# Latent queries and keys of a mixer: one eviction on VectorE, latent keys and values between the latent queries, and the rotation of a head tile in the tick of its norm

## What is computed

```python
proj = h @ w_in
q_g, k_g, v_g, q_lat, kv_lat = jnp.split(proj, IN_OFFSETS, axis=-1)
q_g = apply_rope(rms_norm(q_g.reshape(B, S, 8, 64), gqa_q_norm), cos_g, sin_g)
k_g = apply_rope(rms_norm(k_g.reshape(B, S, 2, 64), gqa_k_norm), cos_g, sin_g)
o_g = blocked_attention(q_g, k_g, v_g)                  # 8 heads over 2 key heads
c_q = rms_norm(q_lat, mla_q_norm)                       # 256 latent features
q_m = (c_q @ w_q_b).reshape(B, S, 8, 96)                # 64 plain + 32 rotated
c_kv = rms_norm(kv_lat[..., :128], mla_kv_norm)
k_rope = apply_rope(kv_lat[..., 128:], cos_m, sin_m)
kv = (c_kv @ w_kv_b).reshape(B, S, 8, 128)              # 64 of key, 64 of value per head
o_m = blocked_attention(q_m, [kv keys, k_rope], kv values)
```

## Time and profile before

| | |
|---|---|
| median of 3 runs | 2328.31 us (2326.7 to 2329.49) |
| profiled execution, first to last instruction (span) | 2324.8 us |
| median of the runs less that span (start and end around it; the profile gives no further time of its execution) | 3.5 us |
| TensorE busy | 2281.0 us, 98% of the span |
| VectorE busy | 1332.0 us, 57% |
| ScalarE busy | 879.5 us, 38% |
| GpSimd busy | 230.2 us, 10% |
| mean granted TensorE clock | 0.995 |

### The profile page before, as it was taken

How to read it: one execution, slowest core, us unless ns; L and a number is a source line. 1 busy time by engine, 2 the same in 40 slices (tenths; PEclk the granted TensorE clock), 3 DMA queues, 4 the chain that set the end, 5 groups by cost and what they waited for, 6 DMA issues and landing times.

```text
span 2324.8 us, 28515 instructions
## 1 busy us (share of the span) xinstructions
PE 2281.0 (98%) x10988; PEld 1640.0 (71%) x10988; DVE 1332.0 (57%) x2055; ACT 879.5 (38%) x1518; POOL 230.2 (10%) x190
## 2 busy tenths in 40 slices
PE   8999999999999999999999999999999999999998
PEld 7755876344675587644467788888888778888886
DVE  5676654233667665432357657777335665877722
ACT  4475542121447554221142234444223234444321
POOL 2212201000221220100000010000001002000000
PEclk9999999999999999999999999999999999999999
DMA  5301439999530143999963233333334423333331
GB/s 178 97 6 39 169 142 388 410 410 410 193 102 5 35 138 145 383 410 410 410 269 109 79 93 91 100 100 92 99 100 136 114 68 91 102 97 100 103 97 46
DMA packets 112085, 381.62 MB, mean 164 GB/s; under 512 B 16464, under 2 KB 17232, under 8 KB 111696
## 3 DMA queue, kind: packets, MB, share of 16 engines
q1 hardware_dynamic: 108208, 366.80, 44.9%
q0 software_dynamic: 2304, 8.39, 0.9%
q10 hardware_dynamic: 1440, 4.62, 0.5%
HBM read 363.51 MB, written 6.29 MB: 159 GB/s over the span
## 4 chain that ended last, share of the span: by engine, by line
PE 88%; DVE 6%; ACT 3%; DMA 1%; POOL 1%; issue 1%; SPq 0%; POOLq 0%; DVEq 0%; ACTq 0%
PE ps L1361 11%; PE ps L1363 11%; PE ps L1362 11%; PE ps L1668 9%; PE ps L1385 5%; PE ps L1387 5%; PE ps L1386 5%; PE ps L1690 5%; PE ps L1549 3%; PE ps L1405 3%; PE ps L1404 3%; PE ps L1406 3%; PE ps L1499 2%; PE ps L1507 2%; PE ps L1700 1%; PE ps L1701 1%
## 5 line engine op out<-in xcount | busy, mean ns | idle before, releaser
L2480 DVE TENSOR_TENSOR wlo<-stage,whi 128x1024 fp32r<-128x1024 f32 x262 | 329.4, 1261 | 279.0 <-ACT whi L1807 278.4
L1361 PE MATMUL ps<-hTh,whi 128*128 128x512 f32 x1120 | 441.1, 394 | 0.0
L1363 PE MATMUL ps<-hTh,wlo 128*128 128x512 f32 x1120 | 436.2, 389 | 0.0
L1362 PE MATMUL ps<-hTl,whi 128*128 128x512 f32 x1120 | 436.0, 389 | 0.0
L1807 ACT ACTIVATE whi<-stage 128x1024 fp32r<-128x1024 f32 x262 | 276.0, 1057 | 328.3 <-PE ps L1387 120.6
L1361 PEld LDWEIGHTS ps<-hTh,whi 128*128 128x128 f32 x1120 | 210.3, 188 | 48.1 <-issue 4.7
L1363 PEld LDWEIGHTS ps<-hTh,wlo 128*128 128x128 f32 x1120 | 210.2, 188 | 43.9
L1362 PEld LDWEIGHTS ps<-hTl,whi 128*128 128x128 f32 x1120 | 210.4, 188 | 42.5
L2395 DVE TENSOR_TENSOR ps<-ps,Rs 128x512 f32<-128x512 f32 x124 | 86.1, 699 | 139.2 <-PE ps L1363 125.2
L2398 DVE SCALAR_TENSOR_TENSOR t<-ps,vecs,t 128x511 f32<-128x511 f32 (+1 forms) x176 | 131.1, 745 | 3.8 <-ACT t L1770 0.7
L2395 DVE TENSOR_TENSOR x<-x,ps 128x512 f32<-128x512 f32 x184 | 116.5, 681 | 28.4 <-PE ps L1387 18.0
(11 more groups left out here) (382 smaller groups left out, 4281.5 us busy)
## 6 DMA issues: line engine op xcount, KB each, us to landing
stage<-in_wpk SPq DMA_DIRECT2D x268, 512.0 KB, 3.6
wa<-in_wd SPq DMA_DIRECT2D x56, 512.0 KB, 15.5
wa<-in_wu SPq DMA_DIRECT2D x54, 512.0 KB, 13.0
wa<-in_wg SPq DMA_DIRECT2D x46, 512.0 KB, 13.9
ws<-in_wg SPq DMA_DIRECT2D x26, 512.0 KB, 10.7
ws<-in_wu SPq DMA_DIRECT2D x24, 512.0 KB, 10.8
wr<-in_wg SPq DMA_DIRECT2D x24, 512.0 KB, 15.2
stage<-in_wd SPq DMA_DIRECT2D x22, 512.0 KB, 16.1
```

The source lines that it names most:

```text
L1361: pe.matmul(o, h, ah, start=k == 0, stop=False)
L1362: pe.matmul(o, h, al, start=False, stop=False)
L1363: t = pe.matmul(o, lo, ah, start=False, stop=k == 7)
L2480: ve.tensor_tensor(M.wlo[i % NW][:, :], M.stage[i % NSTAGE][:, :], f(M.whi[i % NW][:, :]), ALU.subtract).then_inc(*S.wlo.mark(("w", i)))
```

## The change

Chunk 12 is split, and its load issued, before the tick that norms q1 instead of after it. The order of the latent part becomes: two latent queries, a tick, the four key pairs, two value tiles, a tick, two value tiles, two latent queries, a tick, two latent queries, a tick, one latent query, high part of key head 0, the last latent query, low part and copy of key head 0. A latent query is evicted by one VectorE instruction over all 128 partitions; the table `mcs` gets ones in its upper half once. The rotation of k, q0, q1 and q2 goes into `last` instead of `later`. The cosine product on GpSimd is a step of its own right behind the swap, with two buffers in turn. Key head 0 is no longer split behind the first two score tiles.

```diff
-EARLY = {0: ("k", 0), 1: ("k", 0), 2: ("q0", 0), 3: ("q0", 0), 4: ("q0", 1), 5: ("q0", 1), 6: ("k", 1), 7: ("k", 1)}
+EARLY = {2: ("q0", 0), 3: ("q0", 0), 4: ("q0", 1), 5: ("q0", 1), 6: ("k", 1), 7: ("k", 1)}
...
                     self.do("head_swap", l, tile)
+                    self.do("head_cos", l, tile)
...
                     if tile == "q3":
                         self.last.append(lambda: self.last.append(lambda: self.last.append(st3)))
                     else:
-                        self.later.append(st3)
+                        self.last.append(st3)
...
         self.do("point", "hdone", l)
+        i0, i1 = self.chunk(1), self.chunk(1)
         self.do("mk_rope", l, 0)
         self.tick()
...
-        i0, i1 = self.chunk(1), self.chunk(1)
-        for h in range(8):
+
+        def latent_q(h):
             u = self.take()
             self.do("mq", l, h, u, i0, i1)
             self.drop(u)
-            if h in (1, 4, 7):
-                self.tick()
-        self.rel |= {i0, i1}
+        latent_q(0)
+        latent_q(1)
+        self.tick()
         i = self.chunk(0)
         for p in range(4):
             u = self.take()
             self.do("mk", l, p, u, i)
             self.drop(u)
-        self.tick()
         for p in range(1, 4):
             self.do("mk_rope", l, p)
         for m in range(NT):
             u = self.take()
             self.do("vm", l, m, u, i)
             self.drop(u)
+            if m == 1:
+                self.tick()
         self.rel.add(i)
+        for h in range(2, 8):
+            latent_q(h)
+            if h in (3, 5):
+                self.tick()
+            if h == 6:
+                self.do("head_hi", l, "k", 0)
+        self.do("head_lo", l, "k", 0)
+        self.do("key_dup", l, 0)
+        self.rel |= {i0, i1}
...
-        elif name == "mq":
-            l, h, u, i0, i1 = a
-            q.wait_ge(*S.pe.at("mq", l, h))
-            copy(M.mq[0:64, h, :], M.ps[u[0]][0:64, :], ("mq", l, h), ("free",) + u, scale=96 ** -0.5)
...
-            if i:
-                q.wait_ge(*S.dve.at("head_rot", l, HEADS[i - 1]))
-            gp.tensor_tensor(M.tmp[3][:, :], M.raw[SLOT[tile]][:, :], M.cosg[:, :], ALU.mult).then_inc(
+            if i > 1:
+                q.wait_ge(*S.dve.at("head_rot", l, HEADS[i - 2]))
+            else:
+                q.wait_ge(*S.dve.at("krope", l))
+            gp.tensor_tensor(M.tmp[2 + i % 2][:, :], M.raw[SLOT[tile]][:, :], M.cosg[:, :], ALU.mult).then_inc(
...
+            if l == 0:
+                ve.memset(M.mcs[0:64, :], 1.0).then_inc(*S.dve.mark(("mcs",)))
...
-            stt(M.mq[64:128, h, :], M.ps[u[0]][64:128, :], 96 ** -0.5, M.mcs[64:128, :], ALU.mult, ALU.mult, ("mq", l, h),
-                ("free",) + u)
+            q.wait_ge(*S.dve.at("mcs"))
+            stt(M.mq[:, h, :], M.ps[u[0]][:, :], 96 ** -0.5, M.mcs[:, :], ALU.mult, ALU.mult, ("mq", l, h), ("free",) + u)
```

More of the change, by code:

```diff
@@ L1492, in pe_program @@
                 g = 2 * (p - 4) + h
-                q.wait_ge(*S.act.at("mq", l, g))
                 q.wait_ge(*S.dve.at("mq", l, g))
@@ L2208, in pool_program @@
             power(M.st[:, 16 + 4 * g:20 + 4 * g], 4, ("pow", l, "o%d" % g))
-        elif name == "head_rot":
+        elif name == "head_cos":
             l, tile = a
@@ L2592, in dve_program @@
             after_own()
-            tt(M.raw[s][:, :], M.tmp[3][:, :], M.sq[s][:, :], ALU.add, ("head_rot", l, tile))
+            tt(M.raw[s][:, :], M.tmp[2 + HEADS.index(tile) % 2][:, :], M.sq[s][:, :], ALU.add, ("head_rot", l, tile))
         elif name == "head_lo":
```

## The result

The changed kernel takes 2351.3 us (median; 2348.3 to 2355.8) where the kernel before takes 2327.5 us beside it: a ratio of 1.0101, interval 1.0089 to 1.0113. The forecast was 2348.3 us and slower. The profiled execution took 2348.34 us with a span of 2346.3 us, 21.5 us more than before; the other runs have spans of 2348.7 to 2353.8.

A forecast was written before the change was run, and what follows sets the result against it. TensorE, busy 98% of the span, was taken as the bound. Span 2324.8 plus 3.5 around it plus (9.5 - 1.2) x 2 = 16.6 gave 2344.9; a clock fall of 3.4 made 2348.3 us, range 2338 to 2356.

The forecast's parts named there:

- The sum: Whole kernel: scores 9.5 us later, less 1.2 us from the key head, in 2 layers, plus 3.4 us of clock.
- Steps 1 and 2: Layer 0, swaps of k and q0: VectorE waits 3.9 us each; TensorE loses nothing, then 0.6 us in latent query 0.
- Step 3: Layer 0, chunk 12's split ahead of norm q1: norm starts at 89.85, TensorE idles 2.7 us before the transposes.
- Step 4: Layer 0, swap of q1 behind a load and key copy: starts at 91.0, landed at 94.9; norm q2 at 97.6.
- Steps 5 and 6: Layer 0, value tiles wait for banks; tile 3 idles TensorE 4.5 us behind q2's swap; scores begin at 113.45, 9.5 us later.
- The clock: Latent part: idle TensorE brings one fall to 0.50 in each layer, costing 1.7 us a layer, 3.4 us in all.
- The key head: Start of the scores: splitting key head 0 ahead of them gains 1.2 us a layer, bounds 0.5 and 2.0.
- The evictions: Latent queries: dropping ScalarE's 16 halves and widening VectorE's instruction to 128 partitions is worth nothing.
- The clock holds: Rival for the latent part: no fall of the clock, all else as forecast, 2344.9 us; chance 0.31.
- Only q1 and q2 show: Rival: the early two swap waits are absorbed, norm q1 comes at 87.4, stall 2.45 us smaller, 2340.0 us; chance 0.10.
- The banks hide it: Rival: TensorE's eight banks hide the swap waits, 4.4 us faster, 2323.9 us; chance 0.05.
- no difference: Rival: a swap near 2 us in the new place, 3.2 us slower in all, 2331.5 us; chance 0.06.

The follow-up runs named there:

- The late split: Changed kernel with chunk 12 split after the tick that norms q1, as before the change; rotations stay in the tick of their norm: 2342.4 us, ratio 1.0064.

## Why the prediction was right, by its steps

**The sum.** Forecast: (9.5 - 1.2) x 2 + 3.4 = 20.0 us on the span. Measured: 10.6 + 11.6 later scores, less 1.07 + 1.09, is 20.1. The span is 1.5 us above the 2344.8 that this makes of it; the median lies 3.0 us above the forecast, as the profiled execution was the quickest of the four. Two of the other three executions show a mean granted clock of 0.990 and 0.991, this one 0.994, so more time at the low clock may be part of that; they have no trace, and it stays open. The total is closer than its terms, which err in both directions; that they cancel is luck.

**Steps 1 and 2** hold. Norm k ends at 72.47 and its swap has landed at 76.48, 4.0 us; q0's took from 80.36 to 84.33, the same 4.0, against the 3.9 assumed. TensorE feels nothing of the first and 0.35 us of the second, for 0.6.

**Step 3** holds: chunk 12's high part stands in front of norm q1, which starts at 90.32 (forecast 89.85, in an execution 0.9 us later), and the transposes wait 2.05 us. Of the 0.65 us between that and the forecast's 2.7, 0.2 is that the forecast counted from the slot of the last matmul and not from its end; the rest is that norm q1 came 4.5 us after latent query 0 and not 4.9. The late split, 9 us quicker, shows what this edit costs beside the early rotations.

**Step 4** is the term that was mis-sized. The queue was read rightly, the issue came at 91.66 behind the key's copy, but "has landed at 94.9" priced the landing like that of a swap with no transfer of size shortly ahead. With a load of 512 KB 1.2 us and a copy of 256 KB 0.75 us ahead, it took 5.3 us from the first issue and not 3.9 (4.7 in layer 1). Value tile 0 waits 3.80 us for 2.6, but only 1.60 in layer 1, where the key pairs ahead of it ran at the low clock and took 1.6 us longer. The Trainium skill's DMA: Bandwidth & Descriptors, in "Issuing engines are not separate DMA queues", says that all DMAs run on the same 16 engines and interleave; the trace agrees in so far as a 64 KB DMA lands after 3.8 us in that stretch, where the median over all swaps is 2.1.

**Steps 5 and 6** hold in kind. Tile 3 waits for a key pair's copy behind q2's swap, 2.33 us in layer 0 and 4.39 in layer 1, for 4.5. Layer 1:

```profile
694.34 0.50 PE L1488 MATMUL ps<-whi,ckh 128*128 128x512 f32 x1 [1.60 <-DVE mq L2407]
...
701.73 0.47 PE L1488 MATMUL ps<-whi,ckh 128*128 128x512 f32 x1 [4.39 <-DVE mk L2624]
```

From latent query 0 to value tile 3 it is 20.7 and 20.1 us, for 19.6: steps 1 to 6 come out 1.1 and 0.5 us too short. That q2's rotation takes this wait with it was shown by moving it alone.

**The clock** fell in each layer, as forecast, but longer than forecast in layer 0 (for 6.8 us) and twice in layer 1:

```profile
97.90:101.30 3.40, 2.20 (x5) 1.81 (x6) 2.74 (x5) 0.51 (x1) 0.92 (x1) 0.52 0.00 0
101.30:104.70 3.40, 2.87 (x9) 1.75 (x8) 0.56 (x1) 1.18 (x3) 0.48 (x1) 0.50 0.49 115
688.40:691.80 3.40, 3.40 (x10) 2.64 (x9) 0.00 (x0) 1.78 (x3) 1.64 (x1) 0.52 0.78 235
702.00:705.40 3.40, 3.40 (x10) 2.57 (x9) 2.16 (x4) 1.11 (x2) 1.13 (x1) 0.53 0.38 79
```

The granted clock is the column before the last two. The fall in layer 0 (the first two rows) and the first one in layer 1 cost nothing, because what TensorE did slowly there ended in a wait for VectorE anyhow. Only the last lies on dense work: from value tile 3 to the scores 10.56 us, against 8.93 in layer 0 (forecast 8.9), 1.6 us. So 1.6 us in all for a forecast of 3.4, and these 1.8 us too many cancel the 1.6 us by which steps 1 to 6 fell short. The reason given for the falls, idle time of TensorE beside dense work, fits; that a fall in front of a wait is free was the prediction's lower bound and not its forecast.

**The key head** gives 1.07 and 1.09 us, for 1.2; its early split alone, in the kernel before, gave 0.8. **The evictions** and the memset give nothing, as taken.

**The rivals.** *The clock holds* is out by the rows above. *Only q1 and q2 show* is out too: norm q1 came at 90.32, where it wanted 87.4 (88.3 with the later start). *The banks hide it* and *no difference* needed a swap below 1.4 or near 2 us. With one DMA of four the swaps of q0 and q2 took 2.0 us from the norm's end and the loss was still 10 us, more than the (2.8 - 1.2) x 2 that the prediction gave for a swap of 2.0. But q1's took 5.0 there and the clock fell twice, so four swaps of 2.0 us were never run and that point of the prediction stays untested.

## What to carry to other kernels

A transfer that an engine's own instruction asks for should be waited for after that engine's other ready work, not next in line: the wait holds everything behind it, and here such waits cost 12 us over two layers in the old order, 15 in the new one, and 24 with a weight split moved in front of one of them. The Trainium skill's DMA: Bandwidth & Descriptors says the same in its "Rules for kernel authors" (issue early, compute, wait late), and the runs agree. Price a landing by what else is on the DMA engines at that moment, and a slower clock only where no wait follows.

## What the runs showed of the hardware

- A swap of four 64 KB issues on SP was used 4.0 us after the norm in the changed kernel for k and q0, for q0 with a load of 512 KB issued 1.2 us before it. For q1, with a load and a copy of 256 KB close by, it took from first issue to use 5.15 to 5.3 us in layer 0 and 4.7 to 6.0 us in layer 1 of five kernels; a single 64 KB DMA in its place took 4.4 and 4.6 us instead of 2.0.
- The granted clock fell to 0.50 beside gaps of TensorE of 2.0 to 6.0 us, not beside every such gap (the 2.05 us before 91.46 left it at 1.00, the same gap in layer 1 did not), and a fall cost between 0 and 2.8 us, by what lay in it.
- An elementwise instruction of VectorE took 692 ns on 64 partitions and 684 ns on 128 with 512 elements each, both from PSUM.
